# Full-height decay products in a state-space step, their moving operand masked in halves into three buffers

## The chip, the core and the metric

One program runs on one core of a Trainium2 chip. TensorE, VectorE (DVE in the rows), ScalarE (ACT), GpSimd (POOL) and the DMA queue issued from SyncE (SP) each take their instructions in the order of the program and meet at semaphores only. The metric is the device time of one execution in microseconds; less is better.

## The reference, cut to what matters

The program is one inference step of a two-layer backbone over 384 tokens, 128 of context and 256 of latents, in float32. Each layer mixes tokens by pooling, by windowed attention and by a bidirectional state-space scan, and ends in an MLP. The change lies in the scan. For a chunk of 128 tokens and a head with decay logs `a`:

```python
acum = jnp.moveaxis(jnp.cumsum(dtc * A.reshape(G, HG), axis=2), 2, -1)
seg = jnp.where(causal, acum[..., :, None] - acum[..., None, :], -jnp.inf)
w_intra = cb[:, :, :, None] * jnp.exp(seg)
y_diag = jnp.einsum('bcghij,bcjghp->bcighp', w_intra, dtx)
```

`seg` holds, for each pair of tokens (i, j) of the chunk, the difference of two running sums; its exponent weighs the products C·B, and the weighted matrix multiplies the inputs. There are 16 heads in two groups of 8, three chunks and two directions. `new_state_ssd` is the state after the context.

## The kernel before, in words

Weights stream through eight buffers of SBUF; ScalarE rounds each (line 1107), VectorE subtracts the rounded part from the whole (line 1518), and TensorE takes three products for each tile (lines 679 to 681), so that a product in a fast format keeps float32's precision. TensorE's order is written out by hand: large products called fillers stand between the small steps of attention and scan.

**The scan** runs per layer `l` over two groups of heads `g`. Its differences come from a product: the stationary part `acs_row` has, for each of six pairs `i` of chunk and direction, 128 columns of tokens on 128 rows; the rows are four blocks of 32, one for each set of four heads, and group `g` uses the blocks that start at row 64g and 64g + 32. The moving part `spread` holds `acs_col` copied for four heads, each copy masked so that a row keeps only its own head's columns; `own_head` is the mask, four columns of the constant `slot`. The function `seg(g, i)` (lines 914 to 923) multiplies, for `half` 0 and 1, 32 rows by 512 columns into a bank each of the PSUM tensor `seg_ps`. It waits for `seg_taken` (`seg_ps` was read) and for `spread_ready`, and the second product signals `seg_done`. Below, a segment is one call of `seg`; there are 6 for each group, 24 in all.

**GpSimd** makes `spread` in `spread_rows(g, i)` (lines 2044 to 2049): one 128x512 product for all rows, in place `i % 2` of two. From the third on it waits until the segment two back is done. GpSimd's order is also written out. For group `g` it is: `spread_rows` of pairs 0, 1 and 2; the weightings `to_end` (line 2057, into `dtxd`) number 1 and 2; pair 3; the products `skip_rows` 0 and 1 (line 2057 also); pair 4; weighting 3; pair 5; weighting 4; `skip_rows` 2. In the first group pairs 0 and 1 stand ahead of the wait for `wdec_ready` at line 2054. Weighting 4 waits for `aux_done` of the second `state_sum`.

**TensorE's order around it**, for each group (lines 966 to 1007), with its fillers left out where they don't matter:

```python
seg(g, 0)
first_mod2("fill", (13, 22)[g])
transposes4(1, stage[:, 1])
seg(g, 1)
...
seg(g, 2)
ydiag(g, 0)
state_sum(3, 2)
seg(g, 3)
state_sum(4, 1)
seg(g, 4)
end_state(5, 0)
ydiag(g, 1)
seg(g, 5)
end_state(6, 1)
```

`first_mod2` is work of layer 0 alone (line 717, products of 128 rows by 32 columns). Fillers of 24 products stand after `seg(g, 1)`, ahead of `ydiag(g, 0)`, and on both sides of `state_sum(4, 1)`. `ydiag(g, t)` (line 933) multiplies the weighted matrix of chunk t into `ybank`; it waits for `w_ready` and, from the second on, for `y_free`: VectorE must have read the last result out of `ybank`.

**VectorE** takes the other direction of a pair out of `seg_ps` in `pick` (line 1829), weighs in `weigh` (line 1836), subtracts weights (1518), gates outputs (1767, 1786), and adds `ybank` to the skip product in `y_diag` (line 1867), which frees `ybank`. For t = 0 that step waits until all four weightings of its group are done, since it writes over the rows of `xbuf` that weightings 3 and 4 read:

```python
dve.wait_ge(dtxd_ready, (l * 2 + g) * 4 + (4, 2, 1)[t])
nc.vector.tensor_tensor(xbuf[:, t, cols], dtx[:, (g + t) % 2, :], ybank, ALU.add).then_inc(y_free, 1)
```

**ScalarE** copies `seg_ps` into `ew` (line 1368), takes the exponent (1374), and empties the bank `aux`.

Of the kernel before, what the change touches and what calls it, by code (L numbers as in the profile page):

```python
# [15 lines left out]
F32 = mybir.dt.float32  # L16
F32R = mybir.dt.float32r
ALU = mybir.AluOpType
# [4 lines left out]
P = 128  # L23
# [8 lines left out]
HD = 64  # L32
# [140 lines left out]
CONST = {}  # L173
_c = 0
for _name, _n in (("ident", P), ("upper", P), ("lower", P), ("ones", P), ("mask1", P), ("mask2", P),
                  ("rope", 2 * 2 * HD), ("edge", 4 * 16), ("comb", 16), ("eps", 1), ("slot", 10), ("after", P)):
    CONST[_name] = (_c, _c + _n)
    _c += _n
CONST_COLS = _c
# [2 lines left out]
def constants():  # L182
    out = np.zeros((P, CONST_COLS), np.float32)
    r = np.arange(P)

    def put(name, value):
        a, b = CONST[name]
        out[:value.shape[0], a:b] = value.reshape(value.shape[0], -1)

    put("ident", np.eye(P, dtype=np.float32))  # L190
    put("upper", (r[:, None] <= r[None, :]).astype(np.float32))
    put("lower", (r[:, None] >= r[None, :]).astype(np.float32))
    put("ones", np.ones((P, P), np.float32))
    put("mask1", np.where(r[None, :] <= r[:, None], 0.0, NEG).astype(np.float32))
    put("mask2", np.where(r[None, :] >= r[:, None], 0.0, NEG).astype(np.float32))
    nf = HD // 4
    inv = (np.float32(ROPE_BASE) ** (-np.arange(nf, dtype=np.float32) / np.float32(nf))).astype(np.float32)
    rope = np.zeros((P, 2, 2, HD), np.float32)
    for t in range(2):
        pos = t * P + r  # L200
        for half, at in enumerate((pos // GRID_W, pos % GRID_W)):
            ang = at.astype(np.float32)[:, None] * inv[None, :]
            c, s = np.cos(ang), np.sin(ang)
            rope[:, t, 0, half * 32:half * 32 + 32] = np.concatenate([c, c], 1)
            rope[:, t, 1, half * 32:half * 32 + 32] = np.concatenate([-s, s], 1)
    put("rope", rope)
    edge = np.zeros((P, 4, 2, 8), np.float32)
    for g, w in enumerate(WINDOWS):
        for i in range(8):
            edge[:, g, 0, i] = w / (min(i + w // 2, CTX) - max(i - w // 2, 0))  # L210
            at = CTX - 8 + i
            edge[:, g, 1, i] = w / (min(at + w // 2, CTX) - max(at - w // 2, 0))
    put("edge", edge)
    put("after", (r[:, None] > r[None, :]).astype(np.float32))
    put("eps", np.full((P, 1), EPS, np.float32))
    kinds = np.zeros((6, 8), np.float32)
    kinds[:, 0:4] = ((1, -1, -1, 1), (0, 1, 0, -1), (0, 0, 1, 1), (1, 1, 0, 0), (1, 1, 0, 0), (0, 0, 1, 1))
    put("slot", np.concatenate([kinds[:, r % 32 // 4].T, (r[:, None] % 4 == np.arange(4)[None, :]).astype(np.float32)], 1))
    put("comb", np.tile(np.kron(np.eye(8), [[1, 0], [0, 1], [1, 0], [0, 1]]), (4, 1)).astype(np.float32))
    return out  # L220


def backbone_step(nc, consts, x_prompt, x_sample, cache_k, cache_v, state_ssd, c, c_ctx, w_mod, b_mod, norm1_g,
# [26 lines left out]
    with ExitStack() as ctx:  # L250
# [56 lines left out]
        def const(name):  # L307
            a, b = CONST[name]
            return cst[:, a:b]
# [3 lines left out]
        edge = const("edge").rearrange("p (g e i) -> p g e i", g=4, e=2)  # L313
        comb, eps = const("comb"), const("eps")
        hi_part, full_part, keep_row, unit_row, keep_col, unit_col = (const("slot")[:, i:i + 1] for i in range(6))
        own_head = const("slot")[:, 6:10]
        backward = const("after").bitcast(mybir.dt.int32)
        tri = (upper, lower)
        qkT_at = (ybank, aux, ybank, aux, ybank)
# [30 lines left out]
        adt_slots = tb[:].rearrange("p a b -> p (a b)")[:, 0:6 * P]  # L350
        acs_part = tb[:].rearrange("p a b -> p (a b)")[:, 0:6 * P]
        log_slots = tb[:].rearrange("p a b -> p (a b)")[:, 6 * P:12 * P]
        spread = blo_low[:].rearrange("p k t -> p (k t)")[:, 0:8 * P].rearrange("p (b h i) -> p b h i", b=2, h=4)
        ytmp = tb[:].rearrange("p a b -> p (a b)")[:, 0:512]
        def columns(l):

# [105 lines left out]
        def tm_cols(i):  # L462
            return slice(i * P, (i + 1) * P)
# [178 lines left out]
        def _(pe):  # L642
# [15 lines left out]
            for l in range(DEPTH):  # L658
# [255 lines left out]
                def seg(g, i):  # L914

                    if i or g:
                        pe.wait_ge(seg_taken, (l * 2 + g) * 6 + i)
                    pe.wait_ge(spread_ready, (l * 2 + g) * 6 + i + 1)
                    for half in range(2):
                        part = slice(64 * g + 32 * half, 64 * g + 32 * half + 32)  # L920
                        ins = nc.tensor.matmul(seg_ps[:, half, :], acs_row[part, tm_cols(i)],
                                               spread[part, i % 2].rearrange("p h i -> p (h i)"), start=True, stop=True)
                    ins.then_inc(seg_done, 1)

                def ydiag(g, t):
# [1078 lines left out]
        def _(pool):  # L2004
# [18 lines left out]
            for l in range(DEPTH):  # L2023

                for g in range(4):
                    pool.wait_ge(pu_ready, l * 4 + g + 1)
                    if g:
                        pool.wait_ge(pooled_ready, l * 4 + g)
                    u = pu[:, g, :]
                    link(nc.gpsimd.tensor_tensor(pwin[:, 0, 1:PPW], u[:, 0:PPW - 1], u[:, 1:PPW], ALU.add))  # L2030
                    lo, hi, shift = 1, PPW, 1
                    for level in range(1, g + 1):
                        lo, hi = lo + shift, hi - shift
                        a, b = pwin[:, (level - 1) % 2, :], pwin[:, level % 2, :]
                        link(nc.gpsimd.tensor_tensor(b[:, lo:hi], a[:, lo - shift:hi - shift], a[:, lo + shift:hi + shift], ALU.add))
                        shift *= 2
                    s = pwin[:, g % 2, :]

                    for a, b in ((8, 8 + CTX), (16 + CTX, 16 + T)):
                        ends = s[:, a:b].rearrange("p (e i) -> p e i", i=8)[:, ::(b - a) // 8 - 1, :]  # L2040
                        ins = nc.gpsimd.tensor_tensor(ends, ends, edge[:, g], ALU.mult)
                    ins.then_inc(pwin_ready, 1)

                def spread_rows(g, i):

                    if i >= 2 or g:
                        pool.wait_ge(seg_done, (l * 2 + g) * 6 + i - 1)
                    nc.gpsimd.tensor_tensor(spread[:, i % 2], acs_col[:, i, :].bitcast(F32).unsqueeze(1).to_broadcast([P, 4, P]),  # L2048
                                            own_head.unsqueeze(2).to_broadcast([P, 4, P]), ALU.mult).then_inc(spread_ready, 1)

                pool.wait_ge(rows_ready, l * 2 + 2)
                spread_rows(0, 0)
                spread_rows(0, 1)
                pool.wait_ge(wdec_ready, l + 1)

                def weighted(dst, values, g, t):
                    return nc.gpsimd.tensor_tensor(dst.rearrange("p (h d) -> p h d", d=HD),
                                                   xbuf[:, t, g * 512:g * 512 + 512].rearrange("p (h d) -> p h d", d=HD),
                                                   values.unsqueeze(2).to_broadcast([P, HG, HD]), ALU.mult)

                def skip_rows(g, t):

                    n = g * 3 + t
                    if t == 0:
                        pool.wait_ge(skip_ready, l * 2 + g + 1)
                    if n >= 2:
                        pool.wait_ge(y_free, l * 6 + n - 1)
                    weighted(dtx[:, n % 2, :], skips[:, g, t, :], g, t).then_inc(xd_ready, 1)

                for g in range(2):  # L2070
                    def to_end(buf, t, e, n):

                        if n is not None:
                            pool.wait_ge(aux_done, (l * 2 + g) * 11 + n)
                        a = t * 32 + e * 16 + g * 8
                        weighted(dtxd[:, buf, :], wdec[:, a:a + 8], g, t).then_inc(dtxd_ready, 1)

                    if g:
                        spread_rows(g, 0)
                        spread_rows(g, 1)  # L2080
                    spread_rows(g, 2)
                    to_end(0, 2, 1, None if g == 0 else -11 + 6)
                    to_end(1, 1, 0, None if g == 0 else -11 + 7)
                    spread_rows(g, 3)
                    skip_rows(g, 0)
                    skip_rows(g, 1)
                    spread_rows(g, 4)
                    to_end(0, 0, 0, 4)
                    spread_rows(g, 5)
                    to_end(1, 0, 1, 5)  # L2090
                    skip_rows(g, 2)

                square_sum(l, 1)
                if l + 1 < DEPTH:
                    square_sum(l + 1, 0)
# [25 lines left out]
```

## Time and profile before

| what | value |
|---|---|
| time, median of 3 runs | 1463.12 us (1463.06 to 1463.29) |
| the profiled execution's own time | 1463.45 us |
| span of its profile, first to last instruction | 1461.6 us |
| TensorE busy | 1432.1 us, 98% |
| VectorE busy | 882.4 us, 60% |
| ScalarE busy | 658.7 us, 45% |
| GpSimd busy | 119.9 us, 8%, of which line 2048 has 29.7 us in 24 products |

A row of the timeline gives start and length in us, the engine (PE is TensorE's products, PEld its weight loads), the line of the kernel, what is written and read, the shape, and how many such instructions were merged; in brackets stands the engine's idle time before it and whose end ended it. A product's start is the time at which it begins on the array, and its length holds the way through the array, so neighbouring products overlap in the rows: the distance of two starts is what a product costs.

### The profile page before, as it was taken

What the parts mean: (1) busy time and instruction counts of PE and PEld (TensorE: products, weight loads), DVE (VectorE), ACT (ScalarE), POOL (GpSimd) and SP (SyncE); (2) the same over time, 40 slices, a digit from 0 to 9 for tenths busy, and PEclk for the clock granted to TensorE, in tenths of its full rate; (3) what the DMA queues carried; (4) which work ended last, traced back from release to release, by engine and by line L of the source; (5) the groups of instructions that cost most, each with busy time, mean ns of one, the idle gap of its engine ahead of it and who ended that gap; (6) DMA issues with size and microseconds to landing.
All of it is one profiled execution on the core that took longest, in us unless ns stands there. A gap on an engine that the chain in (4) does not pass through costs nothing.

```text
span 1461.6 us, 21008 instructions
## 1 busy us (share of the span) xinstructions
PE 1432.1 (98%) x8329; PEld 1315.8 (90%) x8329; DVE 882.4 (60%) x1465; ACT 658.7 (45%) x1166; POOL 119.9 (8%) x118
## 2 busy tenths in 40 slices
PE   5999999999999999999999999999999999999998
PEld 2899788888899999999988997899889999999998
DVE  3686656674566646454656975567646675556563
ACT  3656554333635525242537575543436453434352
POOL 1000202230001000000010011031300010000000
PEclk9999999999999999999999999999999999999999
DMA  9566425454435656755535432323243434344341
GB/s 337 176 199 193 130 73 159 145 158 132 143 116 153 219 191 198 236 198 191 186 91 178 128 104 71 100 74 116 84 119 115 126 120 130 117 129 129 118 130 44
DMA packets 187336, 210.27 MB, mean 144 GB/s; under 512 B 10798, under 2 KB 156006, under 8 KB 187238
## 3 DMA queue, kind: packets, MB, share of 16 engines
q1 hardware_dynamic: 187238, 208.93, 45.8%
q8 instruction: 66, 1.08, 0.3%
q14 instruction: 32, 0.26, 0.0%
HBM read 204.97 MB, written 3.93 MB: 143 GB/s over the span
## 4 chain that ended last, share of the span: by engine, by line
PE 88%; DVE 6%; ACT 2%; DMA 1%; issue 1%; SPq 1%; ACTq 0%; DVEq 0%
PE bank L679 23%; PE bank L680 23%; PE bank L681 23%; PE bank L695 3%; PE bank L696 3%; PE bank L697 3%; DVE tb L1636 2%; PE y_ps L933 1%; DMA raw<-in_w_mod_dram 1%; DVE wlo L1518 1%; PE bank L717 1%; PE seg_ps L717 1%; PE y_ps L834 1%; PE y_ps L964 1%; PE seg_ps L818 1%
## 5 line engine op out<-in xcount | busy, mean ns | idle before, releaser
L1518 DVE TENSOR_TENSOR wlo<-raw,whi 128x1024 fp32r<-128x1024 f32 (+1 forms) x288 | 352.0, 1229 | 234.2 <-ACT whi L1107 232.8
L679 PE MATMUL bank<-ahi,whi 128*128 128x384 f32 (+1 forms) x1280 | 442.6, 346 | 0.4 <-DVE wlo L1518 0.4
L1107 ACT CAST whi<-raw 128x1024 fp32r<-128x1024 f32 (+1 forms) x288 | 296.1, 1035 | 306.4 <-PE bank L681 159.6
L680 PE MATMUL bank<-alo,whi 128*128 128x384 f32 (+1 forms) x1280 | 432.9, 338 | 0.0
L681 PE MATMUL bank<-ahi,wlo 128*128 128x384 f32 (+1 forms) x1280 | 432.8, 338 | 0.0
L679 PE MATMUL bank<-bhi,whi 128*128 128x384 f32 x768 | 263.6, 343 | 0.0
L680 PE MATMUL bank<-blo,whi 128*128 128x384 f32 x768 | 259.4, 338 | 0.0
L681 PE MATMUL bank<-bhi,wlo 128*128 128x384 f32 x768 | 259.4, 338 | 0.0
L679 PEld LDWEIGHTS bank<-ahi,whi 128*128 128x128 f32 x1280 | 241.3, 188 | 12.2 <-issue 9.2
L680 PEld LDWEIGHTS bank<-alo,whi 128*128 128x128 f32 x1280 | 241.4, 189 | 3.0 <-issue 2.4
L681 PEld LDWEIGHTS bank<-ahi,wlo 128*128 128x128 f32 x1280 | 241.1, 188 | 0.0
L679 PEld LDWEIGHTS bank<-bhi,whi 128*128 128x128 f32 x768 | 144.2, 188 | 6.3 <-issue 4.5
L680 PEld LDWEIGHTS bank<-blo,whi 128*128 128x128 f32 x768 | 144.3, 188 | 1.0 <-issue 1.0
L681 PEld LDWEIGHTS bank<-bhi,wlo 128*128 128x128 f32 x768 | 144.2, 188 | 0.0
L1945 DVE SCALAR_TENSOR_TENSOR xT<-bank,modc,xT 128x128 f32<-128x128 f32 (+1 forms) x160 | 59.2, 412 | 83.3 <-PE bank L681 83.3
L1477 ACT ACTIVATE tb<-tb,small 128x128 f32<-128x128 f32 (+1 forms) x128 | 51.3, 448 | 91.1 <-DVE tb L1976 91.1
L695 PE MATMUL bank<-whi,ahi 128*128 128x512 f32 (+1 forms) x192 | 73.3, 382 | 5.1 <-DVE alo L1551 3.4
L696 PE MATMUL bank<-whi,alo 128*128 128x512 f32 (+1 forms) x192 | 72.0, 375 | 0.0
L697 PE MATMUL bank<-wlo,ahi 128*128 128x512 f32 (+1 forms) x192 | 72.0, 375 | 0.0
L1636 DVE SCALAR_TENSOR_TENSOR tb<-arena_s,pcol,tb 128x386 f32<-128x386 f32 x96 | 59.6, 631 | 14.5 <-ACT tb L1221 12.0
L695 PEld LDWEIGHTS bank<-whi,ahi 128*128 128x128 f32 x192 | 37.3, 194 | 13.0 <-DVE alo L1551 3.5
L2048 POOL TENSOR_TENSOR blo<-bhi,cst 128x512 fp32r<-128x512 f32 x24 | 29.7, 1245 | 198.7 <-DVE bhi L1818 140.4
(244 smaller groups left out, 1368.9 us busy)
## 6 DMA issues: line engine op xcount, KB each, us to landing
raw<-in_w_mlp_dram SPq DMA_DIRECT2D x128, 512.0 KB, 3.6
raw<-in_w_in_dram SPq DMA_DIRECT2D x104, 512.0 KB, 3.8
raw<-in_w_mod_dram SPq DMA_DIRECT2D x88, 512.0 KB, 6.7
raw<-in_w_ssd_o_dram SPq DMA_DIRECT2D x16, 512.0 KB, 3.5
raw<-in_w_out_dram SPq DMA_DIRECT2D x16, 512.0 KB, 3.4
raw<-in_w_pool_o_dram SPq DMA_DIRECT2D x8, 512.0 KB, 3.7
raw<-in_w_attn_o_dram SPq DMA_DIRECT2D x8, 512.0 KB, 3.6
arena_s<-in_w_mod_dram SPq DMA_DIRECT2D x6, 512.0 KB, 6.9
```

Source lines behind the costliest of these rows:

```text
L679: nc.tensor.matmul(dst, uh[:, k, tm_cols(m)], hi[k0 + k], start=first and k == 0, stop=False)
L680: nc.tensor.matmul(dst, uh[:, k, tm_cols(m)], lo[k0 + k], start=False, stop=False)
L681: ins = nc.tensor.matmul(dst, ul[:, k, tm_cols(m)], hi[k0 + k], start=False, stop=last and k == 3)
L695: nc.tensor.matmul(dst, ahi[a][:, tm_cols(t)], uh[:, k, :], start=kq == 0 and k == 0, stop=False)
L696: nc.tensor.matmul(dst, alo[a][:, tm_cols(t)], uh[:, k, :], start=False, stop=False)
L697: ins = nc.tensor.matmul(dst, ahi[a][:, tm_cols(t)], ul[:, k, :], start=False, stop=kq == 3 and k == 1)
L1107: nc.scalar.copy(dst, src).then_inc(hi_ready, 1)
L1477: ins = nc.scalar.activation(row[:, c:d], tb[:, k % 2, c:d], ACT.Relu, bias=hbias[:, k % 2, v:v + 1])
L1518: nc.vector.tensor_tensor(rest, full, top.bitcast(F32), ALU.subtract).then_inc(lo_ready, 1)
L1636: ins = nc.vector.scalar_tensor_tensor(row, src[:, w:w + CVW], convw[:, w, j:j + 1], row, ALU.mult, ALU.add)
L1945: ins = nc.vector.scalar_tensor_tensor(xT[:, k, a:b], psum[:, a:b], modc[:, gain + k, v:v + 1], xT[:, k, a:b], ALU.mult, ALU.add)
L2048: nc.gpsimd.tensor_tensor(spread[:, i % 2], acs_col[:, i, :].bitcast(F32).unsqueeze(1).to_broadcast([P, 4, P]), own_head.unsqueeze(2).to_b ...
```

## The change

The mask is now made for each block of 32 rows: 16 columns in place of 4, so that the constant `slot` has 22 columns instead of 10. GpSimd makes the moving part once for each half, with zeros in all rows outside that half's block, in three places used in turn; each half product of `seg` then takes all 128 rows, and waits for its own half of the moving part. The half number n of a layer and group counts from 0 to 11 for six pairs; a half waits for the last segment that read its place. The order of calls on every engine stays as it was. The whole diff:

```diff
@@ -173,7 +173,7 @@
 CONST = {}
 _c = 0
 for _name, _n in (("ident", P), ("upper", P), ("lower", P), ("ones", P), ("mask1", P), ("mask2", P),
-                  ("rope", 2 * 2 * HD), ("edge", 4 * 16), ("comb", 16), ("eps", 1), ("slot", 10), ("after", P)):
+                  ("rope", 2 * 2 * HD), ("edge", 4 * 16), ("comb", 16), ("eps", 1), ("slot", 22), ("after", P)):
     CONST[_name] = (_c, _c + _n)
     _c += _n
 CONST_COLS = _c
@@ -215,7 +215,8 @@
     put("eps", np.full((P, 1), EPS, np.float32))
     kinds = np.zeros((6, 8), np.float32)
     kinds[:, 0:4] = ((1, -1, -1, 1), (0, 1, 0, -1), (0, 0, 1, 1), (1, 1, 0, 0), (1, 1, 0, 0), (0, 0, 1, 1))
-    put("slot", np.concatenate([kinds[:, r % 32 // 4].T, (r[:, None] % 4 == np.arange(4)[None, :]).astype(np.float32)], 1))
+    put("slot", np.concatenate([kinds[:, r % 32 // 4].T, ((r[:, None] % 4 == np.arange(16)[None, :] % 4)
+                                                         & (r[:, None] // 32 == np.arange(16)[None, :] // 4)).astype(np.float32)], 1))
     put("comb", np.tile(np.kron(np.eye(8), [[1, 0], [0, 1], [1, 0], [0, 1]]), (4, 1)).astype(np.float32))
     return out
 
@@ -313,7 +314,7 @@
         edge = const("edge").rearrange("p (g e i) -> p g e i", g=4, e=2)
         comb, eps = const("comb"), const("eps")
         hi_part, full_part, keep_row, unit_row, keep_col, unit_col = (const("slot")[:, i:i + 1] for i in range(6))
-        own_head = const("slot")[:, 6:10]
+        own_head = const("slot")[:, 6:22].rearrange("p (n h) -> p n h", h=4)
         backward = const("after").bitcast(mybir.dt.int32)
         tri = (upper, lower)
         qkT_at = (ybank, aux, ybank, aux, ybank)
@@ -350,7 +351,7 @@
         adt_slots = tb[:].rearrange("p a b -> p (a b)")[:, 0:6 * P]
         acs_part = tb[:].rearrange("p a b -> p (a b)")[:, 0:6 * P]
         log_slots = tb[:].rearrange("p a b -> p (a b)")[:, 6 * P:12 * P]
-        spread = blo_low[:].rearrange("p k t -> p (k t)")[:, 0:8 * P].rearrange("p (b h i) -> p b h i", b=2, h=4)
+        spread = blo_low[:].rearrange("p k t -> p (k t)")[:, 0:12 * P].rearrange("p (b h i) -> p b h i", b=3, h=4)
         ytmp = tb[:].rearrange("p a b -> p (a b)")[:, 0:512]
         def columns(l):
 
@@ -915,11 +916,11 @@
 
                     if i or g:
                         pe.wait_ge(seg_taken, (l * 2 + g) * 6 + i)
-                    pe.wait_ge(spread_ready, (l * 2 + g) * 6 + i + 1)
                     for half in range(2):
-                        part = slice(64 * g + 32 * half, 64 * g + 32 * half + 32)
-                        ins = nc.tensor.matmul(seg_ps[:, half, :], acs_row[part, tm_cols(i)],
-                                               spread[part, i % 2].rearrange("p h i -> p (h i)"), start=True, stop=True)
+                        n = ((l * 2 + g) * 6 + i) * 2 + half
+                        pe.wait_ge(spread_ready, n + 1)
+                        ins = nc.tensor.matmul(seg_ps[:, half, :], acs_row[:, tm_cols(i)],
+                                               spread[:, n % 3].rearrange("p h i -> p (h i)"), start=True, stop=True)
                     ins.then_inc(seg_done, 1)
 
                 def ydiag(g, t):
@@ -2043,10 +2044,14 @@
 
                 def spread_rows(g, i):
 
-                    if i >= 2 or g:
-                        pool.wait_ge(seg_done, (l * 2 + g) * 6 + i - 1)
-                    nc.gpsimd.tensor_tensor(spread[:, i % 2], acs_col[:, i, :].bitcast(F32).unsqueeze(1).to_broadcast([P, 4, P]),
-                                            own_head.unsqueeze(2).to_broadcast([P, 4, P]), ALU.mult).then_inc(spread_ready, 1)
+                    for half in range(2):
+                        n = ((l * 2 + g) * 6 + i) * 2 + half
+                        if 6 * g + i + half >= 2:
+                            pool.wait_ge(seg_done, (l * 2 + g) * 6 + i - 1 + half)
+                        nc.gpsimd.tensor_tensor(spread[:, n % 3],
+                                                acs_col[:, i, :].bitcast(F32).unsqueeze(1).to_broadcast([P, 4, P]),
+                                                own_head[:, 2 * g + half].unsqueeze(2).to_broadcast([P, 4, P]), ALU.mult)\
+                            .then_inc(spread_ready, 1)
 
                 pool.wait_ge(rows_ready, l * 2 + 2)
                 spread_rows(0, 0)
```

## Rows read from the trace of the kernel before

**Rows 1.** The page's parts 1, 2 and 4: busy time, granted clock, the chain by engine

```profile
PE 1432.1 (98%) x8329; PEld 1315.8 (90%) x8329; DVE 882.4 (60%) x1465; ACT 658.7 (45%) x1166; POOL 119.9 (8%) x118
...
PEclk9999999999999999999999999999999999999999
...
PE 88%; DVE 6%; ACT 2%; DMA 1%; issue 1%; SPq 1%; ACTq 0%; DVEq 0%
```

**Rows 2.** Line 921 alone, TensorE: durations ns min/median/max, first and last start

```profile
L921 PE MATMUL seg_ps<-blo,bhi x48: 489/497/500, 244.6 to 1051.2; 32*128 32x512 f32 x48
```

**Rows 3.** Timeline of TensorE, layer 0: start us, us, engine, line, operation, count

```profile
252.76 0.50 PE L921 MATMUL seg_ps<-blo,bhi 32*128 32x512 f32 x2
253.19 0.44 PE L679 MATMUL bank<-ahi,whi 128*128 128x384 f32 x1
253.47 0.34 PE L680 MATMUL bank<-alo,whi 128*128 128x384 f32 x1
253.65 0.34 PE L681 MATMUL bank<-ahi,wlo 128*128 128x384 f32 x1
```

**Rows 4.** Timeline of all engines, layer 1, first group of heads, around its fifth segment

```profile
991.32 0.34 PE L681 MATMUL bank<-bhi,wlo 128*128 128x384 f32 x1
991.52 0.68 DVE L1867 TENSOR_TENSOR xbuf<-arena_s,y_ps 128x512 f32<-128x512 f32 x1
...
991.59 0.50 PE L921 MATMUL seg_ps<-blo,bhi 32*128 32x512 f32 x2
...
992.02 1.16 PE L950 MATMUL y_ps<-b_tm,arena_s 128*128 128x128 f32 x8
...
993.02 1.90 PE L933 MATMUL y_ps<-xbuf,arena_s 128*128 128x64 f32 x16
```

**Rows 5.** Timeline of TensorE, two neighbouring 128x512 products of the z projection

```profile
362.54 0.39 PE L696 MATMUL bank<-whi,alo 128*128 128x512 f32 x1
362.77 0.39 PE L697 MATMUL bank<-wlo,ahi 128*128 128x512 f32 x1
```

**Rows 6.** Timeline of GpSimd, layer 1, start of the first group

```profile
964.55 2.06 POOL L2048 TENSOR_TENSOR blo<-bhi,cst 128x512 fp32r<-128x512 f32 x2 [70.18 <-DVE bhi L1818]
967.95 1.04 POOL L2048 TENSOR_TENSOR blo<-bhi,cst 128x512 fp32r<-128x512 f32 x1 [1.33 <-PE seg_ps L921]
```

**Rows 7.** Timeline of TensorE, layer 1, the same stretch

```profile
967.30 0.50 PE L921 MATMUL seg_ps<-blo,bhi 32*128 32x512 f32 x2
968.31 0.63 PE L957 MATMUL y_ps<-cst,arena_s 128*128 128x128 f32 x4 [0.51 <-DVE cbs L1883]
968.91 0.50 PE L921 MATMUL seg_ps<-blo,bhi 32*128 32x512 f32 x2
```

**Rows 8.** Timeline of GpSimd, layer 1, the fourth weighting of the first group

```profile
987.51 1.04 POOL L2057 TENSOR_TENSOR arena_s<-xbuf,dts 128x512 f32<-128x512 f32 x1 [3.65 <-PE y_ps L943]
```

**Rows 9.** Timeline of GpSimd, then of VectorE, layer 0, second group

```profile
326.72 1.04 POOL L2057 TENSOR_TENSOR arena_s<-xbuf,dts 128x512 f32<-128x512 f32 x1 [3.65 <-PE y_ps L943]
...
327.90 0.69 DVE L1867 TENSOR_TENSOR xbuf<-arena_s,y_ps 128x512 f32<-128x512 f32 x1 [0.46 <-POOL arena_s L2057]
```

**Rows 10.** Line 1836 alone, VectorE: durations ns min/median/max

```profile
L1836 DVE TENSOR_TENSOR arena_s<-arena_s,cbs x12: 1216/1218/2061, 255.0 to 1057.4; 128x1024 f32<-128x1024 f32 x12
```

**Rows 11.** Timeline of VectorE, GpSimd and TensorE, layer 0, second group, up to line 933

```profile
310.63 3.58 DVE L1518 TENSOR_TENSOR wlo<-raw,whi 128x1024 fp32r<-128x1024 f32 x2 [0.60 <-ACT whi L1107]
...
316.75 1.23 DVE L1836 TENSOR_TENSOR arena_s<-arena_s,cbs 128x1024 f32<-128x1024 f32 x1
...
310.11 3.03 POOL L2057 TENSOR_TENSOR arena_s<-xbuf,skips 128x512 f32<-128x512 f32 x2 [1.74 <-DVE skips L1846]
...
318.03 0.66 PE L933 MATMUL y_ps<-xbuf,arena_s 128*128 128x64 f32 x4 [0.94 <-DVE arena_s L1836]
```

**Rows 12.** Timeline of VectorE, then TensorE, layer 1, second group, the same place

```profile
1033.21 1.95 DVE L1836 TENSOR_TENSOR arena_s<-arena_s,cbs 128x1024 f32<-128x1024 f32 x1
...
1035.27 0.49 PE L933 MATMUL y_ps<-xbuf,arena_s 128*128 128x64 f32 x3
```

## The prediction, made before the change was run

> **What bounds the kernel now.** I read the page first: TensorE is busy 98% of the span, holds 88% of the chain that ended last, and its granted clock is full, 2.4 GHz, wherever the change works [rows 1]. So a nanosecond that a product costs on TensorE counts, and work on another engine counts only where TensorE waits for it. Next I read the line that the change rewrites, then the timelines on both sides of it, looking for two things: what a segment takes out of TensorE's stream, and how late GpSimd could be with its work before TensorE notices.
>
> **A segment on TensorE.** The two half products of 32 rows last 0.50 us each (48 of them, median 497 ns) [rows 2], and the merged row of two is also 0.50 us long [rows 3]: they run side by side on different rows of the array. The next product starts 0.43 us after them (252.76 to 253.19), and the one after that 0.28 us later, where 0.18 us is the usual distance (253.47 to 253.65) [rows 3]: 0.10 us is lost on leaving the 32-row form. On entering it, the pair starts 0.27 us after the last product of a filler (991.32 to 991.59) where 0.18 is usual: 0.09 us is lost [rows 4]. A segment thus takes 0.09 + 0.43 + 0.10 = 0.62 us. Two products of 128 rows by 512 columns, one after the other, cost 2 x 0.23 = 0.46 us, by the distance of two such products of the z projection [rows 5], and lose nothing at the borders, since their neighbours use all rows too. A segment gets cheaper by 0.16 us.
>
> The Trainium skill speaks on both sides here. "TensorEngine Tiling (Array Packing)", section Tiling Modes, says that a change of tiling mode drains TensorE, and that tiles work independently: the trace agrees with both, with the 0.09 and 0.10 us and the shared 0.50 us. By the second rule taken alone, as if the pair cost one product of 0.23 us, the change would add 0.23 us to each of 24 segments, 5.5 us; the rows charge the pair 0.43 us, so I keep the 0.16 us gain.
>
> The gain does not arrive 24 times. Four segments, the fifth of each group, are priced below with their wait. Three in layer 0 (the first of each group, the last of group 0) are followed by products of 128 by 32: a change of form stays, and with 0.09 us for it their sum is 0.46 + 0.09 against 0.09 + 0.43, so +0.03 us each, +0.1 in all. Four stand ahead of a wait for VectorE that takes the gain up: the first of both groups in layer 1, where the transposes wait for line 1883 [rows 7], and the second and third of group 1 in layer 0 [rows 11]. Left are 13 x 0.16 = 2.1 us of gain.
>
> **GpSimd's work doubles.** 24 products of 512 columns become 48; one takes 1.04 us and the next starts 1.00 us after it [rows 6]. I take the same for each half, as shape and types are the same; a dearer mask reading has no row, and the bound is nothing to 0.3 us each, hidden but for four of them. Three half places hold one and a half segments, so the second half of pair i can be made only once segment i - 1 is done. Going through the six:
> - Segment 0 of group 0: both halves take the time that pairs 0 and 1 take now, ending at 966.61 [rows 6]; the segment is at 967.30 [rows 7]. Covered.
> - Segment 1 in layer 1 follows closely. GpSimd starts at 967.95 [rows 6] and ends at 968.99; the first half product can't go before 968.91, as `seg_ps` must be read, the second 0.23 us later. Covered by 0.1 us; without cover it would cost what it is late. In layer 0 the products of line 717 lie between.
> - Segments 2, 3 and 4 have a filler or `ydiag(g, 0)` ahead of them: more than the 1.04 us.
> - Segment 5 has `end_state` and `ydiag(g, 1)` ahead of it. But what is queued behind its half matters.
>
> **The new wait.** The second half of pair 5 waits for segment 4, and GpSimd is in order: weighting 4 stands behind it. Now weighting 4 runs at 987.51, as soon as `state_sum` lets it [rows 8], 4 us before segment 4 at 991.59, and VectorE's line 1867 is at work at 991.52 [rows 4]. After the change, weighting 4 follows segment 4, line 1867 waits for weighting 4, and `ydiag(g, 1)` waits for line 1867. With T the time at which segment 4 could begin (991.32 + 0.18 = 991.50):
> - the second product begins at T + 0.23 and lasts 0.39 [rows 5]: T + 0.62;
> - GpSimd begins 0.15 us after a segment's end (967.80 to 967.95) [rows 6, 7]: T + 0.77;
> - the half, 1.00 to the next start, then weighting 4, 1.04 [rows 6, 8]: T + 2.81;
> - VectorE begins 0.14 us after such an end (327.76 to 327.90) and takes 0.69 [rows 9]: T + 3.64;
> - TensorE begins 0.05 us after VectorE (317.98 to 318.03) [rows 11]: T + 3.69.
>
> Now line 933 begins at 993.02, T + 1.52 [rows 4]. The difference is 2.17 us, gain of the segment included, in every group, as their programs are the same here: 4 x 2.17 = 8.7 us. TensorE has only `end_state` to do in that time. VectorE's weight splits and gated outputs behind line 1867 come 2.9 us later, TensorE about 2.0 us later; so 0.9 us of their slack goes, which I cost at nothing (bound: 0.9 us in each of two groups where a filler follows soon).
>
> **GpSimd against VectorE.** Line 1836 takes 1.22 us, but up to 2.06 us [rows 10], and its long cases lie beside GpSimd's products; two splits of the same width take 3.58 us together beside GpSimd [rows 11]. One meeting costs VectorE up to 0.84 us. The Trainium skill, "SBUF — State Buffer", section SBUF: two separate sides, says that a VectorE operation with two inputs in SBUF and one of GpSimd take turns by an exclusive lock; these rows agree. The change puts three more products of GpSimd ahead of `weigh(g, 0)`. In layer 0, group 1, TensorE already waits 0.94 us for line 1836, which met nothing (1.23 us) [rows 11]: I take two meetings, 1.7 us. In layer 1, group 1, line 1836 ends at 1035.16 and line 933 starts at 1035.27 [rows 12]: one meeting less the 0.1 us between, 0.7 us. In both first groups I take half a meeting, 0.4 us each, for the copy of line 1883 [rows 7] or the weighing. Sum 3.2 us; the bounds are nothing and two meetings in each of four groups, 6.7 us.
>
> The larger constant adds 6 KB to one load at the start, and shifts later tensors by 32 bytes: nothing, or some tenths.
>
> **Sum**, against the profiled execution: 1463.45 + 8.7 - 2.1 + 0.1 + 3.2 = 1473.35 us. That execution lies 0.33 us above the median of the runs shown, so in terms of the median: 1473.0 us.
>
> **Rivals.** *Hidden wait, the other side.* Should GpSimd's second half and weighting 4 fit beside work I have overlooked, then the cheaper segment alone decides: 17 x 0.16 less 0.1, to 20 x 0.16, so -2.6 to -3.2 us, 1460.2 us. It decides if line 1867 starts by T + 0.8, as now. For it speak the border losses; against it that weighting 4 cannot start ahead of T + 1.77 in an in-order queue, 4%. *No change in sum*: the wait costs under 0.6 us a group, because GpSimd's order or its signals are kinder than the code reads: 1463, 4%. *Wait alone*: VectorE absorbs all meetings; 1473.0 - 3.2 = 1469.8 us, 20%. For it: VectorE is busy 60% only [rows 1]. *Chains of lateness*: two meetings everywhere and late splits after the wait, 3.5 + 1.8 more: 1478.3 us, 14%. *The half product is dearer* than line 696's, or the pair loses what running side by side gave (+0.23 for each of 24): up to 1478.5 us, 6%. That the change doesn't do what it says can hardly be: the shapes are plain in the diff.
>
> **How the numbers follow.** The forecast has 52%. The range takes in the wait alone with all gains (1468.5) and the chains of lateness (1479). A measurement of this kernel can tell 0.2%, about 2.9 us. Only the first rival lies beyond that on the fast side, barely: 3%; within 0.2%: 5%; slower: 92%.
>
> **What would show it.** On the changed profile: line 921 with 128 rows, two starts 0.23 us apart, next product with no extra 0.10; 48 products of GpSimd of 1.04 us; TensorE idle about 2 us ahead of line 933 once for each group, ended by line 1867, and line 1867 itself idle until GpSimd's line 2057; line 1836 with more cases near 2 us. I am wrong if line 933 starts by T + 2 after the fifth segment, or if weighting 4 stands ahead of that segment.

## The result, and the profile after

The changed kernel took 1483.66 us (median of four runs, 1482.98 to 1487.06) against 1463.2 us for the kernel before on the same chip: a ratio of 1.0143, interval 1.0131 to 1.0155. It is slower, as forecast, but by 20.4 us where 9.9 was forecast, and outside the range. The profiled execution took 1482.98 us, its span is 1481.2 us. One of all the executions below, 2347.53 us at a mean granted clock of 0.557 in experiment 9, stands apart and is left out of that experiment's figures. The page, parts 1 and 4, then the costliest row of line 2051 in part 5 (busy us and mean ns, then idle time before it):

```profile
PE 1439.2 (97%) x8329; PEld 1325.8 (90%) x8329; DVE 889.2 (60%) x1465; ACT 658.9 (44%) x1166; POOL 150.0 (10%) x142
...
PE 86%; DVE 8%; ACT 2%; DMA 1%; issue 1%; POOL 1%; SPq 1%; ACTq 0%; DVEq 0%
...
L2051 POOL TENSOR_TENSOR blo<-bhi,cst 128x512 fp32r<-128x512 f32 x48 | 58.5, 1231 | 237.3 <-DVE bhi L1819 140.4
```

Against [rows 1], VectorE holds 8% of the chain instead of 6%, and GpSimd is busy 30 us longer, as 24 more products should make it. The lines of the scan have moved: before's 921, 933, 950, 1836 and 1867 are now 922, 934, 951, 1837 and 1868, its 2048 and 2057 are 2051 and 2062. What TensorE waited for (us in total, times, longest), of the whole span:

```profile
PE y_ps L934 <- DVE xbuf L1868: 8.7, 4, 2.2
...
PE y_ps L934 <- DVE arena_s L1837: 3.2, 3, 1.8
...
PE bank L680 <- DVE tb L1768: 0.9, 1, 0.9
...
PE seg_ps L922 <- POOL blo L2051: 0.2, 1, 0.2
```

The same view of before has no wait for line 1867, and this one for line 1836:

```profile
PE y_ps L933 <- DVE arena_s L1836: 0.9, 1, 0.9
```

So the wait that was forecast is there, four times, 8.7 us in all. Here it is in the timeline of all engines, layer 0, first group, behind the fifth segment; these rows answer to [rows 4]:

```profile
268.93 0.63 PE L922 MATMUL seg_ps<-blo,bhi 128*128 128x512 f32 x2
...
269.40 1.08 PE L951 MATMUL y_ps<-b_tm,arena_s 128*128 128x128 f32 x8
...
269.64 1.04 POOL L2051 TENSOR_TENSOR blo<-bhi,cst 128x512 fp32r<-128x512 f32 x1 [6.27 <-PE seg_ps L922]
...
270.64 1.04 POOL L2062 TENSOR_TENSOR arena_s<-xbuf,dts 128x512 f32<-128x512 f32 x1
271.82 0.69 DVE L1868 TENSOR_TENSOR xbuf<-arena_s,y_ps 128x512 f32<-128x512 f32 x1 [2.55 <-POOL arena_s L2062]
```

The half of pair 5 starts right behind the segment; weighting 4 is queued behind it; `y_diag` starts 0.14 us after that. TensorE alone, from the end of this stretch on:

```profile
272.65 2.67 PE L934 MATMUL y_ps<-xbuf,arena_s 128*128 128x64 f32 x16 [2.17 <-DVE xbuf L1868]
275.08 1.20 PE L922 MATMUL seg_ps<-blo,bhi 128*128 128x512 f32 x2
276.21 3.64 PE L718 MATMUL bank<-raw,c 128*32 128x512 f32 x16
```

Here is what I had not forecast. The pair of half products behind the wait lasts 1.20 us, where the same pair takes 0.71 in experiment 2 (below), and the 16 products of line 934 take 2.67 us instead of 1.90 [rows 4]. The windows view shows why (stretch in us, its length, busy us of each engine, then the mean granted clock in the row's third column from the end, as a share of 2.4 GHz):

```profile
240.00:273.70 33.70, 31.17 (x190) 27.44 (x188) 23.80 (x28) 13.70 (x18) 23.43 (x19) 1.00 0.47 141
273.70:280.60 6.90, 6.90 (x31) 3.27 (x30) 4.59 (x7) 1.06 (x1) 4.33 (x4) 0.51 0.19 52
324.90:331.80 6.90, 6.90 (x22) 5.67 (x22) 2.44 (x3) 1.02 (x1) 2.38 (x3) 0.51 0.05 19
345.40:348.80 3.40, 3.40 (x15) 3.31 (x13) 1.95 (x2) 1.32 (x2) 0.00 (x0) 0.50 0.00 0
1069.00:1072.40 3.40, 3.40 (x16) 3.21 (x16) 1.99 (x2) 0.39 (x1) 0.43 (x1) 0.50 0.00 0
```

For about 20.5 us of the two scans the clock is at 1.2 instead of 2.4 GHz; before, it is at 2.4 GHz throughout them. A product is then twice as long, so up to half of that time, some 10 us, is lost. The page's row of the clock shows 9 in every slice, since one slice is 37 us long; the windows are needed to see it. Each stretch begins 1.0 to 2.1 us after an idle time of TensorE has ended: at 272.65 (2.17 us idle), at 323.90 (1.79, the wait for line 1837), at 343.31 (2.20) and at 1067.41 (2.20). A fifth idle time, 2.15 us at 1008.08, was followed by no fall.

That leaves two readings of the 20.4 us. *The clock theory*: 8.7 us of wait for weighting 4, about 3.4 us of waits through contention (3.2 - 0.9 for line 1837, 0.9 for line 1768, 0.2 for line 2051), less the cheaper segments, and all the rest by the clock that falls behind the idle times. *Its rival*: the clock is a companion of little weight, and the time comes from elsewhere, from the full-height products or GpSimd's 24 more. The experiments take one part at a time.

### The profile page after: what moved, and what is told of

The parts are those of the page before. It is cut to its first block, busy times and chain, and to the rows that moved or that the text cites. A ratio compares the mean times of both kernels' runs of the same rounds, so it can differ in the third digit from the quotient of the medians.

```text
span 1481.2 us, 21032 instructions
## 1 busy us (share of the span) xinstructions
PE 1439.2 (97%) x8329; PEld 1325.8 (90%) x8329; DVE 889.2 (60%) x1465; ACT 658.9 (44%) x1166; POOL 150.0 (10%) x142
## 4 chain that ended last, share of the span: by engine, by line
PE 86%; DVE 8%; ACT 2%; DMA 1%; issue 1%; POOL 1%; SPq 1%; ACTq 0%; DVEq 0%
PE bank L680 22%; PE bank L681 22%; PE bank L682 22%; PE bank L696 3%; PE bank L697 3%; PE bank L698 3%; DVE tb L1637 2%; PE y_ps L934 2%; DMA raw<-in_w_mod_dram 1%; DVE wlo L1519 1%; PE bank L718 1%; PE seg_ps L718 1%; PE y_ps L835 1%; PE y_ps L965 1%; PE seg_ps L819 1%
## 5 line engine op out<-in xcount | busy, mean ns | idle before, releaser
L2051 POOL TENSOR_TENSOR blo<-bhi,cst 128x512 fp32r<-128x512 f32 x48 | 58.5, 1231 | 237.3 <-DVE bhi L1819 140.4
L2020 POOL TENSOR_TENSOR arena_g<-tb 128x384 f32<-128x384 f32 x4 | 4.2, 1050 | 499.4 <-ACT tb L1130 499.4
```

What stands on the lines that cost most here:

```text
L2051: nc.gpsimd.tensor_tensor(spread[:, n % 3], acs_col[:, i, :].bitcast(F32).unsqueeze(1).to_broadcast([P, 4, P]), own_head[:, 2 * g + half]. ...
```

## Experiments

Every ratio is against the kernel before, run between on the same chip. Its medians there were 1463.58, 1463.12 and 1462.92 us, so a difference "to before" below is to about 1463.2 us.

**1. Weighting 4 between the two halves of pair 5.** Changed kernel, GpSimd's order alone (`spread_rows` gets the halves as an argument):

```diff
-                    spread_rows(g, 5)
+                    spread_rows(g, 5, (0,))
                     to_end(1, 0, 1, 5)
+                    spread_rows(g, 5, (1,))
```

> The changed kernel with one thing moved in GpSimd's order: weighting 4 stands between the two halves of pair 5, no longer behind the second. Theory (the wait is GpSimd's order, and the idle time lets TensorE's clock fall): the four waits of 2.2 us ahead of ydiag(g, 1) go, 8.7 us, and with them the clock's falls behind them (6.8, 3.4 and 3.4 us at half clock, so about 6.8 us of time); what stays is line 1837's wait in layer 0, group 1, with its own fall (3.4 us of time). 1483.7 - 8.7 - 6.8 = about 1468 us, granted clock up from 0.991 to about 0.995. Rival (the 24 further products of GpSimd cost the time themselves, by holding up VectorE): they are all still there, so the time stays above 1475 us.

Measured: 1467.08 us, ratio 1.0024 (1.0013 to 1.0035). All waits for line 1868 are gone, those for lines 1837 and 1768 stand unchanged (3.2 and 0.9 us), and one stretch of low clock is left, 320.1 to 326.9. The order of two instructions carries 16.6 of the 20.4 us, nearly twice the 8.7 us of wait that it takes away. That stretch of low clock is not in every execution: the mean granted clock is 0.995 in the profiled one (1468.36 us) and one other, and 0.997, as in the kernel before, in the remaining five, the median one among them.

**2. The idle time filled with work.** If the clock is what doubles the wait, then more work for TensorE in that place must make the kernel faster. The four products of `end_state(5, 0)` are done three times, with the same result:

```diff
-                        for j in range(4):
+                        for j in list(range(4)) * (1 if e else 3):
```

> The changed kernel, in which end_state(5, 0) makes its four products three times over (the same values again), so that TensorE has about 2.0 us more work in each of the four waits ahead of ydiag(g, 1), and the wait still ends with line 1868. Theory (the fall of the clock is a cost of its own, beside the wait): line 934 starts as late as before after the fifth segment, its idle time falls from 2.2 to under 0.4 us, the low-clock stretches at 273.7, 345.4 and 1069.0 are gone, and the time falls by about 6.8 us, to 1477 us, by doing more work. Rival (the low clock has another cause than the idle time, or costs nothing): no change or up to 8 us slower, 1483 to 1492 us.

Measured: 1476.06 us, ratio 1.0088 (1.0073 to 1.0103): 7.6 us less than the changed kernel, by 32 more products (the rows count each twice). TensorE in the place shown above:

```profile
269.96 2.89 PE L951 MATMUL y_ps<-b_tm,arena_s 128*128 128x128 f32 x24
273.22 1.97 PE L934 MATMUL y_ps<-xbuf,arena_s 128*128 128x64 f32 x16 [0.36 <-DVE xbuf L1868]
275.00 0.71 PE L922 MATMUL seg_ps<-blo,bhi 128*128 128x512 f32 x2
275.64 1.92 PE L718 MATMUL bank<-raw,c 128*32 128x512 f32 x16
```

Line 934 starts no earlier behind its segment (3.72 us, both times), but from there on everything runs at full speed: line 718 takes 1.92 us where it took 3.64. The profiled execution is the slowest of the four, 1478.8 us, and still has two stretches of low clock, 6.8 us from 321.9 and 3.4 us from 1048.9, both behind waits for line 1837. The mean granted clock rose from 0.991 to 0.996 in the median execution; at half clock half of the time is lost, so 0.005 of mean clock in 1480 us is about 7.4 us, an estimate from rounded figures that agrees with the 7.6 gained. The rival has no room for this: to turn idle time into busy time is worth nothing unless the idle time itself does harm.

**3. Halves of 32 rows again, the rest as changed.**

```diff
+                        part = slice(64 * g + 32 * half, 64 * g + 32 * half + 32)
-... acs_row[:, tm_cols(i)], spread[:, n % 3]
+... acs_row[part, tm_cols(i)], spread[part, n % 3]
```

> The changed kernel with the segments' products back on 32 rows (moving part still made in halves in three places, all waits as in the change). Theory (a segment of 128 rows costs 0.16 us less than a pair of 32, where nothing absorbs it): about 2 us slower than the change, 1485.7 us; line 922 with two starts side by side where both halves are ready. Rival (the two forms cost the same, since the pair runs side by side): no difference, within 0.5 us; rival 2 (running side by side was worth more than the borders cost): faster than the change by up to 5 us.

Measured: 1488.28 us (1482.7 to 1490.54), ratio 1.0155 (1.0133 to 1.0176). Its profiled execution, the slowest of the four, has 34.1 us of low clock in the scans, among it 10.2 us from 1008.8 on, where the changed kernel had none. So the two kernels differ by which idle times the clock fell behind, and the price of the form can't be read from them. It does show that the full-height form is not needed for the slowdown: with halves of 32 rows it is there too.

**4. The wait alone, in the kernel before.** There pair 5 is one product of GpSimd in one of two places; the only edit makes it wait for segment 4, as its second half does after the change:

```diff
-                        pool.wait_ge(seg_done, (l * 2 + g) * 6 + i - 1)
+                        pool.wait_ge(seg_done, (l * 2 + g) * 6 + i - 1 + (i == 5))
```

> The kernel before, with one wait made later: spread_rows(g, 5) waits for the fifth segment instead of the fourth; nothing else (24 products of GpSimd, 32-row products, two places). Theory: this wait alone brings the idle time of about 2.2 us ahead of ydiag(g, 1) four times, 8.7 us, and the clock's falls after it, 3 to 14 us at half clock or 1.7 to 7 us of time: 1463.2 + 8.7 + 1.7 to 7, so 1474 to 1479 us, clock about 0.993. Rival (idle time alone, clock unaffected): 1471.9 us. Rival (the doubled work of GpSimd is the cause): 1464 us or less.

Measured: 1484.33 us (1482.51 to 1485.95), ratio 1.014 (1.0125 to 1.0155). One wait, with no product, place or mask changed, gives as much as the whole change. The waits view, then windows around and behind the first of its four idle times, and around the longest stretch:

```profile
PE y_ps L933 <- DVE xbuf L1867: 8.0, 4, 2.0
```

```profile
269.00:274.80 5.80, 3.79 (x30) 3.13 (x28) 2.48 (x4) 1.60 (x2) 3.82 (x3) 1.00 0.34 90
274.80:278.20 3.40, 3.40 (x17) 1.08 (x20) 3.26 (x5) 0.00 (x0) 2.93 (x3) 0.50 0.00 0
...
1001.80:1012.10 10.30, 9.88 (x38) 9.36 (x39) 7.21 (x10) 2.58 (x3) 4.44 (x3) 0.50 0.17 52
```

The low clock adds up to 23.9 us in four stretches, one for each idle time of 2.0 us, worth up to 12 us. My expectation fell short: it took the clock at less than it did.

**5. A fourth place.** With four half places (the fourth in a tensor not in use then), no half waits for the segment just ahead of it, and the order stays as changed:

```diff
-                        if 6 * g + i + half >= 2:
-                            pool.wait_ge(seg_done, (l * 2 + g) * 6 + i - 1 + half)
+                        if 6 * g + i >= 2:
+                            pool.wait_ge(seg_done, (l * 2 + g) * 6 + i - 1)
```

> The changed kernel with four half places instead of three (the fourth in the pooling weights' tensor, which is free in the scan), so that both halves of pair i wait for segment i - 2 as before; GpSimd's order is the change's. Theory (the wait comes from the third place being short by one): pair 5's halves are made ahead of the fifth segment, weighting 4 runs where it ran before, the four waits of 2.2 us and the clock's falls after them go: about 1467 us, as with weighting 4 moved; the wait for line 1837 of about 1.8 us in layer 0 stays, with one fall of the clock. Rival (weighting 4 behind two halves is late in any case): 1475 us or more.

Measured: 1467.95 us, ratio 1.0034 (1.0022 to 1.0046). Level with experiment 1, by the other road, though four of its five executions have a mean granted clock of 0.995, where most of experiment 1 have 0.997: what costs is weighting 4 behind the wait, and either the order or the shortage of places can be mended.

**6. Experiment 1 with 32-row halves.** Here the form can be read, with the wait out of the way. The edit is that of experiment 3.

> Weighting 4 moved as in e1_weigh_first, and the segments' products back on 32 rows. Against e1_weigh_first this is the product's form alone, with little idle time beside it. Theory (a segment on 128 rows costs 0.16 us less, where no wait takes it up, 17 segments): 2.7 us slower than e1_weigh_first, 1469.8 us. Rival (no difference between the forms): within 0.7 us of 1467.1 us. Rival (side by side is worth more): 1464 us or less.

Measured: 1466.69 us, ratio 1.003 (1.0019 to 1.0041): no difference to experiment 1 in the medians (-0.4 us), where 2.7 were expected. In layer 1, where neither has low clock, the stretch from the first segment to the end of the scan takes 103.72 us with 128 rows and 104.45 with 32, a gain of 0.7 us in twelve segments that are each 0.167 us cheaper. The reason, in part: with 32 rows the waits that end on VectorE are shorter: the one at line 1768 0.56 us instead of 0.91, those for line 1837 shorter by 0.36 us, twice. Of these only one, 0.36 us, lies in layer 1. Two of the twelve segments there stand ahead of the waits for line 1884, where the gain is taken up; the rest of the 1.3 us that are missing was not traced. Where VectorE sets when TensorE goes on, the gain of the segments ahead of that place is waited away.

**7. Fewer meetings of GpSimd and VectorE.** On top of experiment 1, the products `skip_rows` 0 and 1 of each group go from behind pair 3 to behind the first half of pair 5.

```diff
-                    skip_rows(g, 0)
-                    skip_rows(g, 1)
                     spread_rows(g, 4)
                     to_end(0, 0, 0, 4)
                     spread_rows(g, 5, (0,))
+                    skip_rows(g, 0)
+                    skip_rows(g, 1)
```

> e1_weigh_first with one thing more moved in GpSimd's order: the products skip_rows 0 and 1 come after the first half of pair 5 instead of after pair 3. Theory (the waits for line 1837 are VectorE held up by GpSimd's products ahead of the weighing): three GpSimd products stand from the first weight split to the weighing in layer 0, group 1, where the kernel before had four and e1 five; line 1837 ends about 1.8 us or more sooner, its wait falls from 1.8 us to 0 to 0.9, the wait for line 1768 goes, and the fall of the clock near 320 us goes: 1467.1 - 2.7 - 3.4 = 1461 us, faster than the kernel before by 2 us, the granted clock 0.997 again. Rival (the wait has another cause, ScalarE's casts): unchanged at 1467 us. Rival (the moved products hold up VectorE where it is needed just as soon): 1465 to 1469 us.

Measured: 1465.58 us (eleven runs), ratio 1.0016 (1.0008 to 1.0025), where 1461 was expected and 1465 to 1469 was the second rival. The wait for line 1837 halves, the scans have no low clock left, but a new wait has come:

```profile
PE y_ps L951 <- DVE arena_s L1861: 1.8, 2, 1.0
...
PE y_ps L934 <- DVE arena_s L1837: 1.6, 3, 0.9
...
PE bank L680 <- DVE tb L1768: 0.9, 1, 0.9
```

The moved products now meet VectorE's state sum (line 1861), and `end_state` waits for it.

**8. The same move in the kernel before.**

> The kernel before with the same move of skip_rows 0 and 1, to behind pair 5; nothing of the change. It tells how much of the last run's time is the move and how much the product's form. Theory: the wait of 0.94 us for line 1836 in layer 0, group 1, goes, 1463.5 - 0.9 = 1462.6 us; the run before, if it is at 1461, keeps 1.5 us from the 128-row form. Rival: the move gives all of it, 1461 us or less.

Measured: 1462.71 us, ratio 0.9997 (0.9989 to 1.0006). The wait of 0.94 us for line 1836 is gone, two of 0.3 us for line 1860 have come. The move alone brings nothing there that the runs can tell; what it mends in experiment 7 came with the change.

**9. The move of experiment 7 in the second group only**, where the long waits for line 1837 are.

> e1_weigh_first, with skip_rows 0 and 1 moved behind the first half of pair 5 in the second group only. In e7_skips_later the move took 0.9 us of the wait for line 1837 in layer 0 and 0.7 us in layer 1, but brought two waits of end_state for line 1861 in the first groups, 0.8 and 1.0 us. Theory (those two waits are the moved products standing beside VectorE's state update of group 0): they go, the waits for line 1837 stay at 0.9 and 0.3 us: 1465.6 - 1.8 = 1463.8 us, level with the kernel before and at best 0.1% faster, no fall of the clock in the scan. Rival (e7's time above forecast is not in the waits): 1465 us or more.

Measured: 1464.0 us (ten executions), ratio 1.0005 (0.9996 to 1.0014). The waits for line 1861 are gone and the rest stands as in experiment 7. This is the best version with full-height products, and it is level with the kernel before: none that was tried beats it.

**10. Experiment 4 with experiment 2's filling.** The kernel before, with the one wait and the repeated products.

> e4_old_late_pair5 (the kernel before with pair 5 waiting for the fifth segment) with end_state(5, 0)'s four products made three times, which fills most of the four waits. Line 933 still starts about 2.0 us late in each group, so the wait's own price stays. Theory (idle time makes the clock fall, beside the wait): no low-clock stretch in the scan, 1463.3 + 8.0 = 1471.3 us, against 1484.3 us without the further products: 12 us less by more work. Rival (the low clock comes from the program's other parts): 1480 us or more.

Measured: 1472.75 us, ratio 1.0064 (1.005 to 1.0077). Four idle times of 0.2 us are left of 2.0, one stretch of low clock (321.4 to 324.8) of four, and 11.6 us less than experiment 4. TensorE in the same place:

```profile
269.49 2.94 PE L950 MATMUL y_ps<-b_tm,arena_s 128*128 128x128 f32 x24
272.66 1.97 PE L933 MATMUL y_ps<-xbuf,arena_s 128*128 128x64 f32 x16 [0.23 <-DVE xbuf L1867]
274.56 0.50 PE L921 MATMUL seg_ps<-blo,bhi 32*128 32x512 f32 x2
274.99 1.92 PE L717 MATMUL bank<-raw,c 128*32 128x512 f32 x16
```

The late weighting by itself, without the clock, costs 9.6 us over before (of which up to 1.7 us is the one fall left); the clock behind it 11.6, or 10.9 when each experiment is taken against the runs of before beside it (1484.33 - 1463.58 and 1472.75 - 1462.92).

## Why the prediction was right and where it was wrong

**What bounds the kernel, and the sentence that failed.** "Its granted clock is full, 2.4 GHz, wherever the change works" was true of the kernel before and was taken over to the changed one. This is the failed step: the new wait was priced at its own length, 4 x 2.17 = 8.7 us, and no term and no rival asked what 2 us of idle time do to a TensorE that had none there. With the products of experiment 2 in the gap, 7.6 us came back; on the old kernel, experiment 10 against 4, 11.6 us. The Trainium skill, "TensorE: Matmul & The Clock Gate", Part 1, on the gate, states the rule that I left out: the array's clock halves when it has been idle, and activity brings it back. The windows agree with the two levels (1.00 and 0.50). By the page's own limit an idle time as short as these would not have called for a fall; the falls measured here decide. The trace of before has the lower level far from the scan only: at its very end, and for 6.8 us from 37.2 on, where an idle time of 3.42 us (for VectorE's line 1551) ends at 37.96; that should have been read as what an idle TensorE gets.

**A segment on TensorE.** Right in its sum. A row of two halves is 0.63 us long in the fifth segment and 0.70 in most others, a single product 0.39, so the two starts are 0.23 us apart in the one, as forecast, and 0.31 in the others. The borders, in the first segments of layer 0 (the products of line 958 ahead, a filler behind; these answer to [rows 3]):

```profile
250.78 0.60 PE L958 MATMUL y_ps<-cst,arena_s 128*128 128x128 f32 x4
251.13 0.70 PE L922 MATMUL seg_ps<-blo,bhi 128*128 128x512 f32 x2
251.68 0.34 PE L680 MATMUL bank<-ahi,whi 128*128 128x384 f32 x1
251.85 0.34 PE L681 MATMUL bank<-alo,whi 128*128 128x384 f32 x1
```

The filler's products stand 0.17 us apart at once: nothing is lost on leaving. From the product ahead of a segment to the second one behind it are 0.744 to 0.753 us, and before 0.911 to 0.924: cheaper by 0.167 us, forecast 0.16. Beside products of 128 by 32 the first segment of each group in layer 0 costs 0.04 us more, forecast 0.03.

**Its gain in the sum.** Mis-sized: 13 x 0.16 = 2.1 us forecast, 8 of the 13 in layer 1 (1.3 us); there experiments 1 and 6 show 0.7 us, and their medians show nothing. I had looked for waits directly behind a segment; waits take up the gain of the segments ahead of them as well.

**"Covered by 0.1 us."** This failed, for segment 1, the second of its six, in the first group of layer 1. Its second half came late from GpSimd (these answer to [rows 7]):

```profile
977.21 7.05 POOL L2051 TENSOR_TENSOR blo<-bhi,cst 128x512 fp32r<-128x512 f32 x6 [70.17 <-DVE bhi L1819]
...
979.77 0.71 PE L922 MATMUL seg_ps<-blo,bhi 128*128 128x512 f32 x2
...
981.58 0.50 PE L922 MATMUL seg_ps<-blo,bhi 128*128 128x512 f32 x1
982.31 0.51 PE L922 MATMUL seg_ps<-blo,bhi 128*128 128x512 f32 x1 [0.23 <-POOL blo L2051]
...
982.84 0.34 PE L681 MATMUL bank<-alo,whi 128*128 128x384 f32 x1
```

The filler's second product in the kernel before:

```profile
969.63 0.34 PE L680 MATMUL bank<-alo,whi 128*128 128x384 f32 x1
```

GpSimd's six halves took 7.05 us where 1.00 us from start to start gives 6.04. From the start of segment 0 to the filler's second product are 3.07 us, before 2.33 (967.30 to 969.63): 0.74 us more where 0.16 less was forecast, though the waits view counts only 0.2 us of it. That GpSimd was held up by VectorE's split at 978.79 is likely and not shown.

**The new wait.** Right in place, length and cause: 2.17 us forecast for each group, 2.15 to 2.20 measured, 8.7 us in sum. Experiments 1 and 5 remove it in two ways and both come to 1467 to 1468 us.

**GpSimd against VectorE.** Right in sum, 3.4 us for a forecast of 3.2, and roughly in place. VectorE in layer 0, second group (answering to [rows 11]):

```profile
312.99 1.18 DVE L1843 TENSOR_TENSOR tb<-cbs,cst 128x384 f32<-128x384 f32 x1
...
315.14 0.97 DVE L1847 TENSOR_TENSOR skips<-skips,bcast 128x24 f32<-128x24 f32 x1
...
321.90 1.95 DVE L1837 TENSOR_TENSOR arena_s<-arena_s,cbs 128x1024 f32<-128x1024 f32 x1
```

Line 1837 takes 1.95 us instead of 1.23, line 1847 0.97 us instead of 0.18, and TensorE waits 1.79 us for them instead of 0.94. The wait for line 1768 (0.9 us) I had no place for. But this term too has a share in the clock: the idle time at 323.90 is followed by 6.8 us at 1.2 GHz.

**The sum put right.** 8.7 us of wait and 7.6 of clock (experiment 2) are 16.3; experiment 1 takes both away at once and gains 16.6. By their granted clocks (0.996 and 0.997) both median executions also have little or nothing left of the fall near 320, so the 7.6 can hold part of that one as well. What is left to before, 3.9 us, has 3.4 of waits by contention in it and about half a microsecond more for segment 1 of layer 1, less the segments' gain. The fall near 320, 6.8 us long in the profiled execution and worth up to 3.4 us, is hardly in it, then. How the 3.9 us divide further stays open.

**The rivals.** None held. "Hidden wait", "wait alone" and "no change" fell with the first view. "The half product is dearer" (up to 1478.5) came nearest in its number, and the segment's price above refutes it. "Chains of lateness" (1478.3) had the wrong mechanism too: meetings everywhere and late splits behind the wait don't show; experiment 2 has full contention and 7.6 us less.

## What to carry to other kernels

A transfer of work into smaller buffers used in turn adds a wait on the last reader, and in an in-order queue everything behind that wait is late too: list what stands behind it, then reorder (experiment 1) or add a place (experiment 5). A wait of TensorE costs its own length and what the clock takes after it, for waits of 2 us here about as much again; look at the windows behind each new idle time, since a page's row of the clock is too coarse to show it. A gain on TensorE counts only up to the next wait that another engine ends.

## What the runs showed of the hardware

- A single idle time of 1.8 to 2.2 us brought TensorE to half clock for 3.4 to 10.2 us in 16 of the 18 cases in the profiled executions: behind four of five in the changed kernel, all five of experiment 3, all four of experiment 4, and the one each of experiments 1, 2 and 5; not behind 1008.08 in the changed kernel and not in experiment 6 (1.79 us at 318.36). The two stretches of 10.2 us, in experiments 3 and 4, began 0.4 us before TensorE resumed, the others up to 2.1 us after. Two falls came behind shorter ones: in experiment 10, 2.2 us after 0.93 us of idle time at 319.18, and in experiment 2, 2.0 us after 1.05 us at 1046.94; the kernel before has an idle time of 0.94 us in the former place [rows 11] and no fall. The same kernel can have a fall in one execution and not in the next (experiment 1). Why some pass without one, and what sets the length, stays open.
- Repeated, useless products in the idle time made the kernel faster, by 7.6 us (experiment 2) and 11.6 us (experiment 10 against 4).
- An operation of VectorE with 24 elements on a row (line 1847) took 0.97 us instead of 0.18, all four times. Each time a product of GpSimd had begun 0.11 us ahead of it, and it ended 0.04 us after that product; before, none stood beside it. So a chain of small steps suffers as well as a large one. The Trainium skill, "SBUF — State Buffer", section SBUF: two separate sides, has the two engines lock each other out of a shared port; the row agrees.
